# Compressed-block hidden products: high and low parts side by side in one 64-column stationary operand, the two halves added on VectorE

## The reference, cut to what matters

```python
def compress(t, pe, w1, w2):                      # t: 256 tokens x 2 heads x 64
    blk = t[:, cidx] + pe[None, None, :, None, :]  # 15 overlapping blocks of 32 tokens
    blk = blk.transpose(0, 1, 3, 2, 4).reshape(B, n_c, Hkv, CMP_BLOCK * Dh)   # 30 rows x 2048
    return jax.nn.silu(blk @ w1) @ w2              # w1: 2048 x 256, w2: 256 x 64
k_cmp = compress(k, pe_k, wk1, wk2)
v_cmp = compress(v, pe_v, wv1, wv2)
```

## Time and profile before

| what | value |
|---|---|
| three runs of the kernel | 1048.26, 1048.6, 1050.24 us; median 1048.6 |
| the profiled execution, its own time | 1047.58 us |
| its span, first to last instruction | 1045.8 us |
| PE busy | 1008.5 us (96%), 4915 matmuls |
| DVE busy | 596.9 us (57%) |
| ACT busy | 498.9 us (48%) |
| mean granted TensorE clock | 0.994 |
| DMA, mean over the span | 170 GB/s |

### The profile page before, as it was taken

One profiled execution on the slowest core, in us unless ns is written; L12 is line 12 of the kernel. 1 busy time (PEld: TensorE's weight loads), 2 busy tenths in 40 slices (PEclk: granted clock), 3 DMA queues, 4 the chain that ended last, 5 costly groups with the idle time before them and its releaser, 6 DMA issues.

```text
span 1045.8 us, 13296 instructions
## 1 busy us (share of the span) xinstructions
PE 1008.5 (96%) x4915; PEld 838.6 (80%) x4915; DVE 596.9 (57%) x893; ACT 498.9 (48%) x770; POOL 53.9 (5%) x112
## 2 busy tenths in 40 slices
PE   8999999999899999999999999999989899999997
PEld 6888888787778888887888888778878778888885
DVE  5655454747866545456645445576568756544543
ACT  6534344647555434435543434466355364343432
POOL 5000000122010000000000000020000010000000
PEclk9999999999999999999999999999989999999999
DMA  9756474350393647465366565526700364646522
GB/s 328 260 169 220 143 238 145 122 183 29 107 296 121 227 138 238 150 212 201 109 211 223 166 195 197 209 85 228 251 1 1 113 210 136 226 163 198 192 90 81
DMA packets 127410, 178.13 MB, mean 170 GB/s; under 512 B 3154, under 2 KB 102596, under 8 KB 127364
## 3 DMA queue, kind: packets, MB, share of 16 engines
q1 hardware_dynamic: 122832, 170.90, 48.6%
q10 hardware_dynamic: 4020, 6.33, 1.8%
q0 software_dynamic: 512, 0.28, 0.1%
HBM read 176.41 MB, written 1.09 MB: 170 GB/s over the span
## 4 chain that ended last, share of the span: by engine, by line
PE 86%; DVE 7%; ACT 3%; issue 2%; DMA 1%; POOL 0%; SPq 0%; DVEq 0%; POOLq 0%; ACTq 0%
PE ps L919 82%; PE ps L1016 2%; DVE w_lo L1321 2%; DMA raw<-in_l_ffn_wu 1%; PE ps L1103 1%; ACT w_hi L654 1%; ACT xt_hi L670 1%; DVE x L1385 1%; PE ps L932 1%; PE ps L956 1%; DVE down_lo L1407 0%; ACT down_hi L726 0%; DVE w_lo L1537 0%; DVE xt_lo L1333 0%; DVE xn L1377 0%
## 5 line engine op out<-in xcount | busy, mean ns | idle before, releaser
L919 PE MATMUL ps<-w_hi,xt_hi 128*128 128x512 f32 (+2 forms) x912 | 358.1, 393 | 11.0 <-DVE w_lo L1321 4.2
L919 PE MATMUL ps<-w_hi,xt_lo 128*128 128x512 f32 (+2 forms) x912 | 352.4, 386 | 0.0
L919 PE MATMUL ps<-w_lo,xt_hi 128*128 128x512 f32 (+2 forms) x912 | 351.9, 386 | 0.0
L1321 DVE TENSOR_TENSOR w_lo<-raw,w_hi 128x2048 fp32r<-128x2048 f32 (+3 forms) x118 | 258.6, 2232 | 88.8 <-ACT w_hi L654 88.7
L654 ACT ACTIVATE w_hi<-raw 128x2048 fp32r<-128x2048 f32 (+3 forms) x118 | 213.8, 1863 | 29.5 <-DMA raw<-in_l_ffn_wu 13.9
L919 PEld LDWEIGHTS ps<-w_hi,xt_hi 128*128 128x128 f32 x912 | 171.4, 188 | 47.0 <-issue 8.9
L919 PEld LDWEIGHTS ps<-w_hi,xt_lo 128*128 128x128 f32 x912 | 171.3, 188 | 35.3
L919 PEld LDWEIGHTS ps<-w_lo,xt_hi 128*128 128x128 f32 x912 | 171.5, 188 | 32.6
L1402 DVE TENSOR_TENSOR ht_lo<-ps,ht_hi 128x512 fp32r<-128x512 f32 x40 | 27.7, 692 | 175.6 <-ACT ht_hi L720 175.6
L720 ACT ACTIVATE ht_hi<-ps 128x512 fp32r<-128x512 f32 x40 | 23.9, 598 | 214.8 <-PE ps L1016 214.8
L919 PE MATMUL ps<-down_hi,ht_hi 128*128 128x512 f32 x320 | 124.9, 390 | 0.0
(11 more groups left out here) (190 smaller groups left out, 804.3 us busy)
## 6 DMA issues: line engine op xcount, KB each, us to landing
raw_down<-in_l_ffn_wd SPq DMA_DIRECT2D x44, 1024.0 KB, 5.0
raw<-in_l_ffn_wg SPq DMA_DIRECT2D x42, 1024.0 KB, 7.3
raw<-in_l_ffn_wu SPq DMA_DIRECT2D x42, 1024.0 KB, 9.8
raw<-in_l_w_in SPq DMA_DIRECT2D x7, 2048.0 KB, 8.8
raw<-in_l_w_out SPq DMA_DIRECT2D x4, 2048.0 KB, 8.6
gpost<-in_l_ffn_post ACTq DMA_DIRECT2D x4, 512.0 KB, 3.7
bias<-bias_rows ACTq DMA_DIRECT2D x1, 2048.0 KB, 9.6
raw<-in_l_nsa_wk SPq DMA_DIRECT2D x1, 2048.0 KB, 8.4
```

The source lines that it names most:

```text
L919: return pe.matmul(dst, lhs, rhs, start=start, stop=stop, skip_group_check=True)
L1321: dve.tensor_tensor(part(w_lo), part(raw), part(w_hi).bitcast(F32), ALU.subtract).then_inc(main_lo, 1)
```

## The change

The stationary operand of a chunk becomes 64 columns wide: columns 0 to 29 hold the high part, columns 32 to 61 the low part, both in `down_hi` (columns 30, 31, 62 and 63 of a chunk hold whatever was there). Two matmuls per chunk replace three: this operand by the weights' high part, and by their low part. Rows 0 to 29 of the result are then high by high plus high by low; rows 32 to 61 are low by high plus low by low (the latter is new). VectorE copies rows 32 to 61 to `logit` slot 2, waits for that, and adds them to rows 0 to 29 into `logit` slot i (`sum_hidden`). Silu on ScalarE then works in place on `logit` and waits for the sum rather than for the product.

```diff
-        def z_part(buf, i):
-            return buf[:, 1024 * i:1024 * i + 480].rearrange("p (m g c) -> p m g c", m=16, g=2)
+        def z_part(i, low):
+            wide = down_hi[:, 1024 * i:1024 * (i + 1)].rearrange("p (m c) -> p m c", c=64)
+            return wide[:, :, 32 * low:32 * low + 2 * NCMP].rearrange("p m (g c) -> p m g c", g=2)
...
-                act.activation(z_part(down_hi, i), z, ACT.Copy).then_inc(z_hi, 1)
+                act.activation(z_part(i, 0), z, ACT.Copy).then_inc(z_hi, 1)
...
-                act.wait_ge(hid_ready, i + 1)
-                act.activation(logit[0:2 * NCMP, i, :], ps[0:2 * NCMP, 2 + i, 0:CMP_HID], ACT.Silu).then_inc(hid_done, 1)
+                act.wait_ge(hid_summed, i + 1)
+                act.activation(logit[0:2 * NCMP, i, :], logit[0:2 * NCMP, i, :], ACT.Silu).then_inc(hid_done, 1)
...
-                    at = 1024 * i + 2 * NCMP * m
+                    both = down_hi[:, 1024 * i + 64 * m:1024 * i + 64 * (m + 1)]
                     cols = slice(m * CMP_HID, (m + 1) * CMP_HID)
-                    ins = three(ps[0:120, 2 + i, 0:CMP_HID], down_hi[:, at:at + 120], down_lo[:, at:at + 120],
-                                w_hi[:, n % 2, cols], w_lo[:, n % 2, cols], m == 0, m == 15)
+                    dst = ps[0:64, 2 + i, 0:CMP_HID]
+                    mm(dst, both, w_hi[:, n % 2, cols], m == 0, False)
+                    ins = mm(dst, both, w_lo[:, n % 2, cols], False, m == 15)
...
-                dve.tensor_tensor(z_part(down_lo, i), z, z_part(down_hi, i).bitcast(F32), ALU.subtract).then_inc(z_lo, 1)
+                dve.tensor_tensor(z_part(i, 1), z, z_part(i, 0).bitcast(F32), ALU.subtract).then_inc(z_lo, 1)
             split_main(n0 + 3)
             turned_plain("kw", 1, lambda k: qk[:, 9, :])
             split_main(n0 + 4)
             dve.wait_ge(q_zeroed, 4)
             turned_by_group("qc")
+
+            def sum_hidden(i):
+                dve.wait_ge(hid_ready, i + 1)
+                dve.tensor_copy(logit[0:2 * NCMP, 2, :], ps[32:32 + 2 * NCMP, 2 + i, 0:CMP_HID]).then_inc(hid_low, 1)
+                dve.wait_ge(hid_low, i + 1)
+                dve.tensor_tensor(logit[0:2 * NCMP, i, :], ps[0:2 * NCMP, 2 + i, 0:CMP_HID], logit[0:2 * NCMP, 2, :],
+                                  ALU.add).then_inc(hid_summed, 1)
+            sum_hidden(0)
...
             dve.memset(vcmp, 0.0).then_inc(vcmp_zero, 1)
             split_main(n0 + 5)
+            sum_hidden(1)
             split_main(n0 + 6)
```

More of the change, by code:

```diff
@@ L294, in trunk @@
         hid_ready, hid_done, hid_turned = sem("hid_ready"), sem("hid_done"), sem("hid_turned")
+        hid_summed, hid_low = sem("hid_summed"), sem("hid_low")
         hid_spread, hid_zero = sem("hid_spread"), sem("hid_zero")
```

## The result

The changed kernel is slower: 1050.48 us (median of 20 runs) against 1047.59 us for the kernel before (median of 20 runs), 2.9 us more. The ratio is 1.0028, with a 95% interval of 1.0020 to 1.0036. In microseconds the interval is 2.1 to 3.8. The prediction was +2.5 us, slower, with 0.60 on that side.

A forecast was written before the change was run, and what follows sets the result against it. VectorE's list was taken to bound TensorE's start of n0+5. Freed matmuls 0, longer list +0.9, clock +1.6 give +2.5 us on the 1048.6 us median: 1051.1 us, range 1048.4 to 1053.3.

The forecast's parts named there:

- What bounds the stage: TensorE's start of n0+5 at 731.97 waits 1.45 us for VectorE's `w_lo`; VectorE's list bounds it, not TensorE's work.
- The freed 3.8 us worth nothing: 32 matmuls fewer in the two rounds save 3.8 us of TensorE time, which becomes idle time: worth 0.
- The longer list: Copy and addition between VectorE's query copies and gates delay n0+5: 0.42 + 0.41 + some 0.07 = 0.9 us.
- Nothing for the late Silu, splits and transfer: Second Silu, split of n0+6 and later loads come later, with slack of 1 us or more each: cost 0.
- The clock: About 5.1 us of idle before n0+5 drops TensorE to half clock for 3.4 us: 1.6 us lost.
- the rival with the longer stretch: Low clock at n0+5 lasts 6.8 us, as at 777.2: 3.2 us lost, +4.1 in all, 1052.7 us; chance 0.20.
- the first rival: Delay of n0+5 without low clock, the gap causing no fall that matters: +0.9, 1049.5 us; chance 0.22.
- The faster rival: Freed TensorE time reaches the end through an earlier start of n0+5: -3.8 us, 1044.8 us; chance 0.08.

The follow-up runs named there:

- Experiment 3: Kernel before with the third product of each chunk (low inputs by high weights) left out, nothing added on VectorE: 1049.95 us, ratio 1.0018.
- experiment 2: Kernel before with one copy and one addition of 30 x 256, result unused, between VectorE's query copies and gates: 1048.35 us, ratio 1.0007.
- Experiment 4: Changed kernel with the first sum moved behind the split of block n0+5, next to the second sum: 1049.28 us, ratio 1.0018.
- experiment 1: Changed kernel with 36 extra products of 256 columns after the second round, filling TensorE's idle time: 1049.03 us, ratio to before 1.0008.
- experiment 6: Changed kernel with the split of block n0+5 moved ahead of both sums, the gates and the clearing: 1048.09 us, ratio to before 1.0007.
- experiment 7: Changed kernel with the split of n0+5 ahead of sums, gates and clearing, plus 20 extra products after the second round: 1047.24 us, ratio 0.9997.
- experiment 5: Kernel before with the split of block n0+5 moved ahead of the gates and the clearing on VectorE: 1047.14 us, ratio 0.9997.

## Why the prediction was right, and where it was off

**What bounds the stage: right.** I read the wait at 731.97 in the earlier trace rows and the chain in the earlier trace rows over the page's 86% of TensorE. Experiment 3 is the direct test: a third of the products less brought no gain.

**The freed 3.8 us worth nothing: right**, and by the path forecast. The first round and the transposes end earlier, a new idle microsecond stands before the second round (0.91 us), and the idle time before n0+5 was put at 5.1 and measured at 4.84 us.

**The longer list: right in place, a little high in size.** 0.9 us forecast; 0.80 us on the list (0.79 in experiment 2) and 0.76 us at TensorE's start, both in the changed kernel and with the two instructions alone. Copy and addition were as read from the earlier trace rows. The 0.07 us that I had added for hand-overs wasn't there: from the start of the copy to that of the gates it is less than 0.42 + 0.41.

**Nothing for the late Silu, splits and transfer: right.** In the changed kernel the second Silu moved as forecast (ScalarE's timeline).

```profile
736.75 0.42 ACT L892 ACTIVATE logit<-logit 30x256 f32<-30x256 f32 x1 [4.74 <-DVE logit L1618]
737.07 3.70 ACT L656 ACTIVATE w_hi<-raw 128x2048 fp32r<-128x2048 f32 x2
```

Its result is there at 737.2, and the transposes that want it come at 741.8. TensorE had no new wait behind n0+5 up to 765 us. Experiment 4 delays the first Silu further at no cost that the trace shows. Part of this cover, 2.4 us, was the low clock's own delay of TensorE; in experiment 1, without it, the transposes came at 739.4 and still didn't wait.

**The clock: right that it falls, too small in size.** This is the term that was mis-sized. "I take **1.6 us**, the shorter stretch, because the work that follows here is dense" took the low stretch for as long as the one at 241.3. The profile of the changed kernel shows the longer one, 6.8 us, of which 5.1 us were work, and 2.4 us lost, between my forecast and the rival with the longer stretch (3.2). The median over 20 runs says 2.9 in all, so about 2.1 us for the clock if the list costs 0.8; that is an estimate, since no run times the list's part clear of noise. The reason given was wrong too: dense work follows in all these kernels, and in four profiles with a fall (the changed kernel and experiments 3, 4 and 6) the stretch lasted 6.8 us three times and 3.4 us once. When the clock falls within or after the idle time differed as well: 1.7 us before the work started in the changed kernel, 1.1 us after it in experiment 3.

**Luck in the number.** The two errors in the difference go opposite ways, 0.1 us too much on the list and some 0.5 too little on the clock, and leave it 0.4 us short. The forecast of 1051.1 us is 0.6 us above the measured 1050.48: its base, the 1048.6 of three runs, was 1.0 us above the median of 20, and the 0.4 that are missing took part of that back. The falls elsewhere in the kernel, 1.6 us each, are larger than either error. The lower end of the range doesn't follow from its own rule, either: half a microsecond below the first rival is 1049.0, not 1048.4.

**The chances.** The first rival, delay without low clock, is what experiment 1 makes by hand. The argument against it, that "both falls followed stretches fuller than the new gap", is weaker than it looks: the same work with TensorE as little busy (1.94 of 3.5 us from 240.0 on) had no fall behind it in the changed kernel. The faster rival is excluded by experiment 3.

By the Trainium skill (TensorE: Matmul & The Clock Gate, "Why this matters for your kernels") idle gaps between bursts of matmuls bring the clock back to half. The traces agree for gaps of 3.00, 3.95, 4.08 and 4.84 us, and experiments 1 and 7 show a clock of 1.00 with the gap filled.

## What to carry to other kernels

Before taking work off the engine that is busiest, look at what releases it next. If that is another engine's list, the freed time only turns into idle time, and an instruction added to that list delays that release by its full length (0.76 us at the start of n0+5 for two instructions of 0.42 and 0.41).

On TensorE longer idle time has a price of its own: here four kernels that freed time (the changed kernel and experiments 3, 4 and 6) lost 1.6 to 2.8 us to the clock in their profiles, and useless products in the gap of two of them (experiments 1 and 7) won it back.

Before two spans are subtracted, follow the lateness from point to point. Here 0.95 us of the 3.5 were there before the change came in, and 0.7 us of the stage's loss came back behind it.

## What the runs showed that I had not expected

- Idle time of over 2 us isn't safe by its length. A gap of 3.00 us had a fall in it (experiment 6), one of 2.21 us had none behind it (experiment 2). But all nine profiles have the same gap of 2.2 us shortly before 25 us, and two of them (the changed kernel and experiment 1) have a fall of 3.4 us there: 1.1 us after the gap's end in the changed kernel, 0.2 us before it in experiment 1. The other seven have none.
- Falls come and go between kernels that do the same work at that point: the one at 241.3 is in five of the nine profiles, the one near 777 in all. Each of the short ones is worth 1.6 us of time, as much as the effects that are looked for.
- How much of the low clock lies on work differs from kernel to kernel with nearly the same idle time: 1.6 us lost after 3.95 us of idle, 2.8 us after 4.08 us. Idle time read from one profile says that a cost is likely, and gives only a spread for its size.
- A stationary operand of 64 columns made the matmuls of 256 columns no faster in a stream than one of 120: 0.117 against 0.12 us.
- The transfer of block n0+5 landed 8.8 to 9.0 us after its issue in the three profiles with three products per chunk (before, experiments 2 and 5) and after 7.7 to 8.0 us in the six with two. Why is not tested. ScalarE starts on the block 7.87 us after the first round does in experiment 7 and 8.74 us in experiment 5, which is why VectorE doesn't wait in the former. The prediction had 8.8 us throughout.
